# Hybrid block front: own banks for chunks 4 to 9, 64-row halves for two small products, and a new VectorE order

## The reference, cut to what matters

```python
proj = hn @ w_in                                   # hn = rmsnorm(h); h is the end of the first block
qa, ka, va, rw = jnp.split(proj, [SB_WIDTH, 2 * SB_WIDTH, 3 * SB_WIDTH], axis=-1)
xm = pf + (shift_right(pf, 1) - pf) * mu           # pf = rw: token shift, mixed with mu
r, k, v, wl, al, gl = jnp.split(xm, [...])
w = -jax.nn.softplus(-(w0 + jnp.tanh(wl) @ w2)) - 0.5     # low-rank product, 64 x 512
decay = jnp.exp(-jnp.exp(w))
a = jax.nn.sigmoid(a0 + al @ a2)                          # low-rank product, 64 x 512
kk = k * ph(k_k)
kk = kk * lax.rsqrt(jnp.maximum(jnp.sum(kk * kk, axis=-1, keepdims=True), 1e-24))
k = k * (1.0 + (a - 1.0) * ph(k_a))
```

## Time and profile before

| | |
|---|---|
| median of 3 runs | 1286.54 us |
| span of the profiled execution, first to last instruction | 1284.3 us |
| what lies around the span (median less span) | 2.2 us |
| TensorE busy | 1264.3 us (98%) |
| VectorE busy | 917.8 us (71%) |
| ScalarE busy | 756.7 us (59%) |
| GpSimd busy | 41.2 us (3%) |
| share of the chain that ended last | TensorE 84%, VectorE 9%, ScalarE 4% |

### The profile page before, as it was taken

One profiled execution on the slowest core, in us unless ns is written; L12 is line 12 of the kernel. 1 busy time (PEld: TensorE's weight loads), 2 busy tenths in 40 slices (PEclk: granted clock), 3 DMA queues, 4 the chain that ended last, 5 costly groups with the idle time before them and its releaser, 6 DMA issues.

```text
span 1284.3 us, 29209 instructions
## 1 busy us (share of the span) xinstructions
PE 1264.3 (98%) x12162; PEld 1232.1 (96%) x12162; DVE 917.8 (71%) x1314; ACT 756.7 (59%) x980; POOL 41.2 (3%) x34
## 2 busy tenths in 40 slices
PE   9999999999999999998999999999999999999997
PEld 8999999998999999998989899999999889999997
DVE  5779887488569887478757388665588779666557
ACT  6667665367657665367555266554475876554444
POOL 1010000010010000000000010000001001000000
PEclk9999999999999999999999999999999999999999
DMA  8465555555345555545401136555534335555520
GB/s 343 170 225 182 202 189 209 189 191 210 119 156 190 197 196 197 196 158 196 165 34 41 64 140 230 196 195 197 187 141 176 132 128 208 198 196 196 196 99 34
DMA packets 31980, 220.61 MB, mean 172 GB/s; under 512 B 3712, under 2 KB 3840, under 8 KB 6160
## 3 DMA queue, kind: packets, MB, share of 16 engines
q1 hardware_dynamic: 30672, 213.36, 46.2%
q0 software_dynamic: 784, 4.85, 1.1%
q10 hardware_dynamic: 432, 1.05, 0.2%
HBM read 218.20 MB, written 1.05 MB: 171 GB/s over the span
## 4 chain that ended last, share of the span: by engine, by line
PE 84%; DVE 9%; ACT 4%; issue 1%; DMA 1%; POOL 0%; SPq 0%; DVEq 0%; ACTq 0%; POOLq 0%
PE ps L1915 21%; PE ps L1917 21%; PE ps L1916 21%; PE ps L1926 16%; DVE w_lo L1127 3%; PE ps L1921 2%; PE ps L1923 2%; PE ps L1922 2%; ACT w_hi L507 1%; DVE xt L1179 1%; PE ps L2140 1%; DVE xA L1190 1%; DMA raw<-stream 1%; DVE xB L1151 0%; DVE xB L1190 0%
## 5 line engine op out<-in xcount | busy, mean ns | idle before, releaser
L1127 DVE TENSOR_TENSOR w_lo<-raw,w_hi 128x2048 fp32r<-128x2048 f32 x197 | 449.6, 2288 | 137.4 <-ACT w_hi L507 137.2
L507 ACT ACTIVATE w_hi<-raw 128x2048 fp32r<-128x2048 f32 x197 | 376.3, 1914 | 157.7 <-PE ps L1917 152.0
L1915 PE MATMUL ps<-xB,w_hi 128*128 128x256 f32 x1120 | 311.0, 278 | 0.5 <-DVE w_lo L1127 0.5
L1916 PE MATMUL ps<-xB,w_hi 128*128 128x256 f32 x1120 | 309.3, 276 | 0.0
L1917 PE MATMUL ps<-xB,w_lo 128*128 128x256 f32 x1120 | 309.2, 276 | 0.0
L1915 PEld LDWEIGHTS ps<-xB,w_hi 128*128 128x128 f32 x1120 | 210.2, 188 | 2.1 <-issue 1.5
L1915 PE MATMUL ps<-xA,w_hi 128*128 128x256 f32 x744 | 208.9, 281 | 2.1 <-DVE gl L1540 1.6
L1916 PEld LDWEIGHTS ps<-xB,w_hi 128*128 128x128 f32 x1120 | 210.3, 188 | 0.1
L1917 PEld LDWEIGHTS ps<-xB,w_lo 128*128 128x128 f32 x1120 | 210.3, 188 | 0.0
L1917 PE MATMUL ps<-xA,w_lo 128*128 128x256 f32 x744 | 205.7, 276 | 0.0
L1916 PE MATMUL ps<-xA,w_hi 128*128 128x256 f32 x744 | 205.7, 276 | 0.0
(11 more groups left out here) (317 smaller groups left out, 1847.8 us busy)
## 6 DMA issues: line engine op xcount, KB each, us to landing
raw<-stream SPq DMA_DIRECT2D x199, 1024.0 KB, 4.8
raw<-stream SPq DMA_DIRECT2D x4, 512.0 KB, 7.4
at_bias<-rel POOLq DMA_DIRECT2D x1, 2048.0 KB, 8.3
hT<-x_t SPq DMA_DIRECT2D x4, 256.0 KB, 6.0
lora_w<-lora POOLq DMA_DIRECT2D x1, 1024.0 KB, 5.1
out_t<-xt SPq DMA_DIRECT2D x4, 256.0 KB, 2.6
hcon<-hyc POOLq DMA_DIRECT2D x1, 576.0 KB, 3.9
wsT<-wst ACTq DMA_DIRECT2D x1, 512.0 KB, 4.8
```

Of the source, the lines that this page charges most:

```text
L507: nc.scalar.activation(w_hi[c.slot][:], raw[c.slot][:], ACT.Copy).then_inc(hi_made, 1)
L1127: nc.vector.tensor_tensor(w_lo[c.slot][:], raw[c.slot][:], w_hi[c.slot][:].bitcast(F32), ALU.subtract).then_inc(lo_made, 1)
L1915: nc.tensor.matmul(out, wh, xh, start=start, stop=False, skip_group_check=True)
L1916: nc.tensor.matmul(out, wh, xl, start=False, stop=False, skip_group_check=True)
```

## The change

Six edits. (1) Chunks 4 to 9 go to banks 4 and 5 in turn. (2) The low-rank products move from behind chunk 4 to behind chunk 5, and each runs over its own 64 rows only, a `w` and an `a` matmul in turn; they go to banks 0 to 3. (3) The cumulative sums move from behind chunk 5 to behind chunk 6, over 64 rows and 128 columns each: half of them there, half after the first of chunk 7's eight steps. (4) GpSimd takes four folds of squares at this norm, VectorE keeps two. (5) VectorE scales chunk 2 together with 0 and 1, makes the `w_lo` of chunk 5 before the shifts, and makes that of chunk 7 before it adds `w0`; later shifts move forward or back by a step. (6) ScalarE rounds chunk 5 before it copies bank 0, and other copies and roundings change places.

```diff
-POOLED = {n: 0 if n == N_HY else 2 if n in FOLDED else 1 for n in range(11)}
+POOLED = {n: 2 if n in FOLDED else 1 for n in range(11)}
@@ hy_bank
-            return g if g < 4 else g % 2
+            return g if g < 4 else 4 + g % 2 if g < 10 else g % 2
@@ GpSimd
+            pool.wait_ge(sq_made, 4 * N_HY + 2)
+            nc.gpsimd.tensor_tensor(xt[:, 0:2, :], xt[:, 0:2, :], xt[:, 2:4, :], ALU.add).then_inc(sq_added, 1)
+            pool.wait_ge(fin_sq, 2)
+            nc.gpsimd.tensor_tensor(slot[2][:, 0:2, :], slot[2][:, 0:2, :], slot[2][:, 2:4, :], ALU.add).then_inc(fin_added, 1)
+            pool.wait_ge(sq_made, 4 * N_HY + 3)
+            pool.wait_ge(sq_added, ADDED_BY[N_HY] + 1)
+            nc.gpsimd.tensor_tensor(xt[:, 0:2, :], xt[:, 0:2, :], xt[:, 4:6, :], ALU.add).then_inc(sq_added, 1)
+            pool.wait_ge(fin_sq, 3)
+            pool.wait_ge(fin_added, 1)
+            nc.gpsimd.tensor_tensor(slot[2][:, 0:2, :], slot[2][:, 0:2, :], slot[3][:, 0:2, :], ALU.add).then_inc(fin_added, 1)
             pool.wait_ge(h_updated, 16)
             pool.dma_start(hcon[:], hyc[:, 2 * P:]).then_inc(hy_landed, 16)
@@ ScalarE, front of the hybrid block
+            split_hi(Chunk(c0 + 2).ahead())
             act.wait_ge(mu_ready, 1)
-            hy_copy(0)
-            hy_copy(1)
-            split_hi(Chunk(c0 + 2).ahead())
-            hy_copy(2)
+            for g in range(3):
+                hy_copy(g)
+            split_hi(Chunk(c0 + 3).ahead())
+            hy_copy(3)
...
-            act.wait_ge(cum_made, 1)
+            hy_copy(6)
+            act.wait_ge(cum_made, 2)
...
@@ VectorE, end of ffn(1)
-                if n + 1 in FOLDED and n + 1 != N_HY:
+                if n + 1 in FOLDED:
                     fold_squares(n + 1)
                 if n + 1 == N_HY:
-                    for b in (0, 4):
-                        dve.wait_ge(sq_made, 4 * N_HY + b // 2 + 2)
-                        own.mark(nc.vector.tensor_tensor(xt[:, b + 2:b + 4, :], xt[:, b + 2:b + 4, :], xt[:, b:b + 2, :],
-                                                         ALU.add))
-                    own.wait()
-                    nc.vector.tensor_tensor(xt[:, 6:8, :], xt[:, 6:8, :], xt[:, 2:4, :], ALU.add).then_inc(sq_folded, 1)
                     dve.wait_ge(fin_sq, 4)
-                    for i in (2, 3):
-                        own.mark(nc.vector.tensor_tensor(slot[i][:, 0:2, :], slot[i][:, 0:2, :], slot[i][:, 2:4, :], ALU.add))
-                    own.wait()
-                    nc.vector.tensor_tensor(slot[2][:, 0:2, :], slot[2][:, 0:2, :], slot[3][:, 0:2, :],
+                    dve.wait_ge(fin_added, 2)
+                    nc.vector.tensor_tensor(slot[2][:, 0:2, :], slot[2][:, 0:2, :], slot[3][:, 2:4, :],
                                             ALU.add).then_inc(fin_folded, 1)
@@ TensorE
+            def cumulate(step):
+                for t in range(2):
+                    for b in range(2):
+                        for hf in range(2):
+                            r, d = slice(64 * hf, 64 * hf + 64), 2 * ((hf + step) % 2) + b
+                            last = plain(half(d, t).rearrange("p (i n) -> p i n", i=2)[:, :, r],
+                                         flat(3)[r, 512 * t + P * d:512 * t + P * d + P],
+                                         h_cum[r].rearrange("p (i n) -> p i n", i=2)[:, :, r])
+                last.then_inc(cum_made, 1)
+            stick_in[7] = {1: cumulate_rest}          # waits cum_made 1, then cumulate(1)
             for g in range(14):
-                if 4 <= g < 6:
-                    pe.wait_ge(hy_mixed, g - 3)
+                if g == 4:
+                    pe.wait_ge(rs_made, N_HY + 1)
...
+                if g == 10:
+                    pe.wait_ge(decay_made, 3)
...
-                if g == 4:
+                if g == 5:
...
-                    for t in range(2):
-                        plain(ps[:, 2 + t, :], wlal[:, P * t:P * t + P], lora_w[:, 0, :]).then_inc(w_proj, 1)
                     for b in range(RBLK):
-                        last = plain(half(4 + b // 2, b % 2), lora_w[:, 1, P * b:P * b + P], wlal)
+                        t, h = divmod(b, 2)
+                        w_last = plain(half(2 + t, h), wlal[0:64, P * t:P * t + P], lora_w[0:64, 0, T * h:T * h + T])
+                        a_last = plain(half(b // 2, b % 2), lora_w[64:128, 1, P * b:P * b + P], wlal[64:128, :])
...
-                elif g == 5:
+                elif g == 6:
                     pe.wait_ge(w_sig, 2)
                     pe.wait_ge(a_sig, 1)
-                    for t in range(2):
-                        for b in range(RBLK):
-                            last = plain(half(2 + b, t), flat(3)[:, 512 * t + P * b:512 * t + P * b + P], h_cum)
-                    last.then_inc(cum_made, 1)
+                    cumulate(0)
```

More of the change, by code:

```diff
@@ L268, in build @@
         gate_half, tail_sq = sem("gate_half"), sem("tail_sq")
-        fin_sq, fin_folded, fin_made, fin_mean, fin_scaled = [
-            sem(n) for n in ("fin_sq", "fin_folded", "fin_made", "fin_mean", "fin_scaled")]
+        fin_sq, fin_added, fin_folded, fin_made, fin_mean, fin_scaled = [
+            sem(n) for n in ("fin_sq", "fin_added", "fin_folded", "fin_made", "fin_mean", "fin_scaled")]
         xt_made = sem("xt_made")
@@ L861, in _ @@
             nc.scalar.activation(gl[:], gl[:], ACT.Sigmoid).then_inc(lora_in, 1)
-            split_hi(Chunk(c0 + 3).ahead())
-            hy_copy(3)
             split_hi(Chunk(c0 + 4).ahead())
@@ L874, in _ @@
             for b in range(RBLK):
-                last = nc.scalar.activation(slot[4][:, b, :], half(4 + b // 2, b % 2), ACT.Sigmoid, bias=col("rw_a0", b))
+                last = nc.scalar.activation(slot[4][:, b, :], half(b // 2, b % 2), ACT.Sigmoid, bias=col("rw_a0", b))
             last.then_inc(a_sig, 1)
@@ L881, in _ @@
             nc.scalar.activation(slot[9][:], slot[9][:], ACT.Exp, scale=-0.5, bias=col("ln256")).then_inc(kk_rn, 1)
-            hy_copy(5)
             split_hi(Chunk(c0 + 6).ahead())
-            act.wait_ge(cum_made, 1)
+            hy_copy(6)
+            act.wait_ge(cum_made, 2)
             decay(5, 1, 1.0)
             decay(6, 0, -1.0)
-            hy_copy(6)
+            hy_copy(7)
             split_hi(Chunk(c0 + 7).ahead())
-            hy_copy(7)
-            split_hi(Chunk(c0 + 8).ahead())
             act.wait_ge(factors, 1)
@@ L893, in _ @@
             hy_copy(8)
+            split_hi(Chunk(c0 + 8).ahead())
             split_hi(Chunk(c0 + 9).ahead())
@@ L1543, in shift @@
                 last.then_inc(hy_mixed, 1)
-            dve.wait_ge(hy_landed, 32)
-            scale_early(N_HY, 0, c0, 0)
-            scale_early(N_HY, 1, c0 + 1, 1)
-            shift(0)
-            shift(1)
-            scale_early(N_HY, 2, c0 + 2, 2)
-            shift(2)
+            for g in range(3):
+                scale_early(N_HY, g, c0 + g, g)
             split_lo(Chunk(c0 + 2).ahead())
-            shift(3)
+            for g in range(4):
+                shift(g)
             dve.wait_ge(hy_mixed, 4)
@@ L1559, in _ @@
             shift(4)
+            split_lo(Chunk(c0 + 4).ahead())
+            dve.wait_ge(hy_landed, 32)
             for t in range(2):
@@ L1562, in _ @@
                 nc.vector.tensor_tensor(flat(3)[:, 512 * t:512 * t + 512], ps[:, 2 + t, :], w0b, ALU.add).then_inc(w_arg, 1)
-            split_lo(Chunk(c0 + 4).ahead())
+            shift(5)
             for b in range(2):
@@ L1569, in _ @@
             split_lo(Chunk(c0 + 5).ahead())
-            shift(5)
             dve.wait_ge(kk_rn, 1)
@@ L1580, in _ @@
                                                 op0=ALU.add, op1=ALU.mult))
+            shift(6)
             dve.wait_ge(hy_mixed, 6)
@@ L1588, in _ @@
             split_lo(Chunk(c0 + 6).ahead())
-            shift(6)
+            shift(7)
             link(nc.vector.tensor_tensor(slot[4][:], slot[4][:], slot[8][:], ALU.mult))
@@ L1594, in _ @@
                 nc.vector.tensor_tensor(slot[dst][:], slot[dst][:], slot[by][:], ALU.mult).then_inc(factors, 1)
-            shift(7)
             split_lo(Chunk(c0 + 7).ahead())
@@ L2191, in stick_scores @@
                 pe.wait_ge(hy_evac, 2 if u < 2 else 4)
-                if u == 0:
-                    pe.wait_ge(decay_made, 3)
-                elif u == 1:
+                if u == 1:
                     pe.wait_ge(bonus_made, 2)
-                else:
+                elif u > 1:
                     pe.wait_ge(arg_made, u - 1)
@@ L2261, in _ @@
                     pe.wait_ge(hy_mixed, 4)
-                    for t in range(2):
-                        plain(ps[:, 2 + t, :], wlal[:, P * t:P * t + P], lora_w[:, 0, :]).then_inc(w_proj, 1)
                     for b in range(RBLK):
-                        last = plain(half(4 + b // 2, b % 2), lora_w[:, 1, P * b:P * b + P], wlal)
-                        if b % 2:
-                            last.then_inc(a_proj, 1)
```

(6 more changed lines are left out.)

6 lines of the change are left out of this document (5 added, 1 removed).

## The result

The changed kernel took 1279.53 us in the median of five runs (1278.34 to 1280.56), the kernel before 1286.54 (1284.91 to 1286.6, five runs in this comparison). The ratio is 0.9944, with a 95% interval of 0.9933 to 0.9955: 7.0 us faster. The forecast was 1280.2, the range 1278.2 to 1283.8.

A forecast was written before the change was run, and what follows sets the result against it. TensorE was taken to set the pace, with VectorE and ScalarE close behind. Terms: 1.6 + 2.4 + 1.8 + 1.5 - 0.4 - 0.3 - 0.3 = 6.3 us, so 1286.5 - 6.3 = 1280.2 us, range 1278.2 to 1283.8.

The forecast's parts named there:

- Chunk 4 in its own bank and the low-rank products later: TensorE's waits ahead of chunk 4 and ahead of the low-rank products go: gains of 1.6 and 2.4 us.
- Low-rank halves: Low-rank products on 64 rows, upper and lower alternating: four pairs cost 1.7 us against 3.52, gain 1.8.
- Cumulative halves: Cumulative sums as eight pairs of 64-row matmuls: 1.8 us against 3.27, gain 1.5.
- the split: Cumulative sums in two parts: one more change back to a chunk and a wait for the first part's results, loss 0.4 us.
- Chunk 8: TensorE waits there 0.2 to 0.4 us for VectorE's shift of chunk 6, same bank; taken as a loss of 0.3.
- The tightest spot: VectorE's shift of chunk 6, due 606.7 against TensorE's 606.5; any lateness of VectorE or ScalarE is lost in full.
- GpSimd's folds: Sum of squares before the hybrid block: four adds on GpSimd, taking turns with VectorE; loss 0.4, taken as 0.3 us.
- The sum of 7.6: Total gain if GpSimd's adds were counted at their free price, gaining 0.8 us instead of the loss.
- the halves don't run together: Rival: upper and lower half matmuls do not overlap, 3.3 us less gain, 1283.5 us; chance 0.08.
- VectorE became no bound: Rival judged: VectorE, with 34.3 us to do, becomes the bound, 2.5 us more late, 1282.7 us; chance 0.14.
- Given back whole: Rival: GpSimd's adds at their worst, 4.2 us lost, and VectorE 2 us late: 1286.1 us, no change; chance 0.08.
- half matmuls stand alone: Rival: each of 24 half matmuls pays 0.35 us for switching halves, 11.7 us more than forecast, 1291.9 us; chance 0.04.

The follow-up runs named there:

- lr_full: The changed kernel with the low-rank products over all 128 rows as before, at their new place; 1280.76 us, ratio 0.9956.
- dve_order: The changed kernel with VectorE's order ahead of the shift of chunk 3 as before; 1282.23 us, ratio 0.9965.
- later: The kernel before with low-rank products and head sums behind chunk 5, cumulative sums behind chunk 6; 1286.18 us, ratio 0.9993.
- cum_full: The changed kernel with the cumulative sums over all 128 rows in one block behind chunk 6; 1280.32 us, ratio 0.9952.
- fold_dve: The changed kernel with all six folds of squares on VectorE, as before; 1280.74 us, ratio 0.9951.
- in_turn_off: The changed kernel with all w products before all a products, all upper cumulative halves before all lower ones; 1282.07 us, ratio 0.9967.

## Why the prediction was right

The mechanisms held, with one term wrong in sign and the others mis-sized by 0.3 us and more. By step:

- **Chunk 4 in its own bank and the low-rank products later: forecast 1.6 + 2.4.** Both waits went, and nothing over 0.32 us took their place. By starts the two are worth 4.3: the first low-rank matmul stood 34.60 us behind chunk 0 before and stands 35.05 behind now, with one more chunk (5.44) ahead of it and 0.66 less at the fold: 34.60 + 5.44 - 0.66 - 35.05 = 4.33. The 0.4 over the table's 3.9 (0.5, if one takes out that the half-row block stands 0.10 later behind chunk 5 than lr_full's full-row one) is what a wait costs beside its idle time: the last record runs on 0.16 us past the next start, and the first records behind the wait come slower (583.52 and 583.74, 0.22 apart, where 0.113 is usual). The experiments put a condition on it that the prediction named only as work to be followed: with VectorE's old order 1.8 of it comes back at chunk 5 (dve_order), and 1.72 at chunk 8 (later).
- **Low-rank halves, 1.8.** Right in kind, measured 1.32 by lr_full. The block is 1.93 us instead of 1.7: eight pairs of records at 0.21, and 0.2 more for its first and last. It stands against 3.45 and not 3.52, since the old block also started slowly behind its wait; the head sums behind it take 1.64 instead of 1.54; and it starts 35.05 behind chunk 0, in lr_full 34.95. That is 3.45 - 1.93 - 0.10 - 0.10 = 1.32.
- **Cumulative halves, 1.5, less 0.4 for the split.** Measured 0.83 by cum_full, where 1.1 was forecast. Each part takes 1.09 us where I had 0.9, again 0.2 for entering and leaving, and there are two of them. The chunks around them come out 0.26 longer, where 0.4 was forecast for the split: 0.15 by the second return to a chunk, 0.10 in chunk 6 ahead of the first part. In both halves steps the mis-sized term is the same: the earlier trace rows gave the price of a pair inside a run of pairs, and I left out the ends of the block.
- **Chunk 8, a loss of 0.3.** There was none. VectorE's shift ended at 606.97, which is 606.20 on the clock of before, where I had 606.7; chunk 8 came at 606.70, where I had 606.5. Both engines were 0.66 us ahead at the fold, and TensorE then came 0.86 later than I had counted from there, by its longer blocks above all, VectorE's chain 0.16 later. The tightest spot had its slack from blocks that were dearer than forecast.
- **GpSimd's folds, a loss of 0.3: wrong in sign.** It is a gain of 0.66 in the front, 0.75 by fold_dve. The failing step is "558.7 + 4 x 1.3 + 4 x 0.4 = 565.5 for the last add". The taking of turns was right, the price of a turn was not. By the records (GpSimd's are rough) the three adds that begin beside a rest of VectorE take 1.48 us and the one that does not takes 1.29: some 0.19 for a turn, three times, where I had 0.4, four times. The four adds take 5.62 us in all and not 6.8, and the last ends at 564.35 on the clock of before, 0.77 us earlier, where I had 565.5. VectorE paid more, 1.7 us, but its folds behind end at 565.63 and 566.23, where I had 566.5 and 567.1. The first sum came 0.40 late, not 1.2. The second had no wait, as forecast, and that gained 1.06 and not 0.8: 0.96 between the starts of the two sums and 0.10 behind the second.

The Trainium skill (SBUF — State Buffer, Who interferes with whom, and the definition of the shared port pair) says that whichever instruction starts first holds the pair to its end and the other is blocked wholly. The trace agrees, in that each of the three rests that begin beside a running add ends only 0.28 us behind it. The prediction charged GpSimd a whole rest of 0.4 at each turn; the measured 0.19 decides. The sum of 7.6 that the prediction gives beside the rule is a slip: with 0.8 gained at the fold in place of 0.3 lost its terms add to 7.4.

Put together by differences of starts: waits 4.33, fold 0.66, low-rank block 3.52 less 1.93, cumulative sums 3.27 less 2.18, head sums -0.10, the chunks around the split -0.26. That is 7.31 of the 7.32 us. Against the forecast's 6.3 the fold gave 1.0 more, the waits 0.3 and chunk 8 0.3, and the halves with their split 0.6 less (2.32 by these differences, 2.9 forecast). That the time came out only 0.7 us off is in part luck, since the errors partly cancelled.

The rivals: that the halves don't run together is excluded by the starts 0.01 apart. VectorE became no bound (30.02 of 32.54 us). "Given back whole" and "half matmuls stand alone" did not come; in_turn_off, where they stand alone, costs 2.1 us and not 11.7, so that price was far too high. Behind chunk 9 the gain stayed, but for the 0.6 us told above, which the prediction put at nothing.

## What to carry to other kernels

Taking away a wait moves the next deadline forward. Where a second engine is busy for 30 of 33 us, look at its order in the same step: here the wait came back one chunk later (dve_order) or at chunk 8 (later). Price an engine's wait by starts and not by the idle time in the table, and look at what the wait does to TensorE's clock: two waits of 1.6 and 2.4 us were harmless here, one of 4.2 us cost 2.7 us more. Two products whose operands fill half the rows each ran wholly in pairs here only when they alternated in the program, and a short block of them cost 0.2 us more than its pairs, and 0.1 to 0.2 more in the work around it.
